# Mamba-2 decay rows read back from DRAM in place of TensorE broadcasts, and a gate moved ahead of two copies

## The reference, cut to what matters

```
adt  = dt * a                      # one value per token and head
a_cs = cumsum(adt, axis=-1)        # inside each chunk of 128
decay  = exp(segsum(adt))          # a_cs[l] - a_cs[s] for l >= s
y_diag = (C B^T * decay) @ xg
states = B @ (xg * exp(a_cs[-1] - a_cs))
y_off  = (C @ previous state) * exp(a_cs)
```

## Time and profile before

| | us |
|---|---|
| median of 3 runs (lowest, highest) | 2133.89 (2132.24, 2136.08) |
| profiled execution: its own time | 2128.42 |
| profiled execution: span of its instructions | 2126.6 |
| PE busy | 1967.8 (93%) |
| DVE busy | 1157.7 (54%) |
| ACT busy | 757.1 (36%) |
| POOL busy | 613.2 (29%) |

### The profile page before, as it was taken

One profiled execution on the slowest core, in us unless ns is written; L12 is line 12 of the kernel. 1 busy time (PEld: TensorE's weight loads), 2 busy tenths in 40 slices (PEclk: granted clock), 3 DMA queues, 4 the chain that ended last, 5 costly groups with the idle time before them and its releaser, 6 DMA issues.

```text
span 2126.6 us, 27616 instructions
## 1 busy us (share of the span) xinstructions
PE 1967.8 (93%) x10964; PEld 982.9 (46%) x10964; DVE 1157.7 (54%) x2320; ACT 757.1 (36%) x1345; POOL 613.2 (29%) x630
## 2 busy tenths in 40 slices
PE   2999889998999999989999899899999999999896
PEld 2443344454444455534444566544444444444542
DVE  6418999999995456422545688620233333332516
ACT  2413444314312866213321344331233333333503
POOL 0022415544446002478311322511101222022240
PEclk8999999999999999999999999999999999999998
DMA  8110111022311002331311100211111011100301
GB/s 336 40 45 25 50 40 50 21 85 75 129 79 69 37 11 85 139 119 40 128 40 40 40 1 1 79 40 40 41 41 41 1 41 41 41 10 32 120 20 79
DMA packets 18225, 127.10 MB, mean 60 GB/s; under 512 B 1744, under 2 KB 1744, under 8 KB 12848
## 3 DMA queue, kind: packets, MB, share of 16 engines
q1 hardware_dynamic: 12720, 97.57, 12.1%
q0 software_dynamic: 5376, 27.76, 3.3%
HBM read 106.45 MB, written 18.87 MB: 59 GB/s over the span
## 4 chain that ended last, share of the span: by engine, by line
PE 75%; DVE 14%; ACT 4%; POOL 3%; DMA 2%; issue 2%; SPq 0%; DVEq 0%; POOLq 0%; ACTq 0%
PE ps L871 48%; PE ps L868 7%; DVE arena L1631 3%; POOL arena L570 2%; PE ps L986 1%; PE ps L1223 1%; PE ps L921 1%; PE ps L963 1%; PE ps L969 1%; PE ps L908 1%; PE ps L1243 1%; PE ps L1088 1%; PE ps L936 1%; DMA W<-in_mods 1%; DVE arena L1847 1%
## 5 line engine op out<-in xcount | busy, mean ns | idle before, releaser
L871 PE MATMUL ps<-hT,W 128*128 128x512 bf16 x3456 | 812.3, 389 | 23.0 <-DVE arena L2150 7.2
L871 PEld LDWEIGHTS ps<-hT,W 128*128 128x128 bf16 x3456 | 327.6, 97 | 465.6 <-issue 34.9
L579 POOL TENSOR_TENSOR W<-W 128x512 bf16<-128x512 f32 x216 | 235.9, 1131 | 459.6 <-DMA W<-in_loads 458.3
L871 PE MATMUL ps<-W,arena 128*128 128x512 bf16 x1152 | 262.4, 388 | 8.8 <-DVE W L2016 6.2
L570 POOL TENSOR_TENSOR arena<-arena 128x512 f32<-128x512 f32 (+1 forms) x80 | 139.7, 1746 | 196.4 <-ACT arena L1569 126.4
L1409 ACT ACTIVATE arena<-arena,small 128x128 f32<-128x128 f32 (+9 forms) x192 | 114.1, 641 | 198.9 <-DVE small L1721 181.9
L871 PEld LDWEIGHTS ps<-W,arena 128*128 128x128 bf16 x1152 | 111.1, 97 | 158.1 <-DVE W L2016 6.7
L1402 ACT ACTIVATE arena<-arena,small 128x128 f32<-128x128 f32 (+9 forms) x192 | 122.8, 640 | 122.8 <-DVE small L1710 87.3
L868 PE MATMUL ps<-arena,W 128*128 128x512 f32 (+1 forms) x320 | 142.0, 598 | 0.9 <-DVE arena L1767 0.9
L871 PE MATMUL ps<-arena,W 128*128 128x512 bf16 x576 | 132.3, 391 | 5.4 <-POOL arena L631 4.4
L1710 DVE CUSTOM_DVE_ANT_0 arena<-ps,arena 128x256 f32<-128x256 f32 (+7 forms) x128 | 62.1, 518 | 123.8 <-PE ps L969 109.4
(11 more groups left out here) (321 smaller groups left out, 2673.7 us busy)
## 6 DMA issues: line engine op xcount, KB each, us to landing
W<-in_loads SPq DMA_DIRECT2D x34, 2048.0 KB, 7.6
gates_scratch<-arena SPq DMA_DIRECT2D x32, 256.0 KB, 2.0
arena<-gates_scratch POOLq DMA_DIRECT2D x2, 4096.0 KB, 15.4
arena<-in_x SPq DMA_DIRECT2D x2, 2048.0 KB, 13.8
W<-in_mods SPq DMA_DIRECT2D x2, 2048.0 KB, 18.4
hT<-in_mods SPq DMA_DIRECT2D x2, 2048.0 KB, 28.8
arena<-in_x POOLq DMA_DIRECT2D x1, 4096.0 KB, 13.5
x_scratch<-arena POOLq DMA_DIRECT2D x8, 512.0 KB, 8.7
```

The lines of the kernel that those rows point to most:

```text
L579: last = nc.gpsimd.tensor_tensor(low(v), v, high(v), ALU.subtract)
L871: last = mm(o, left[:, :, a], right[:, :, b], start=(k == 0 and (a, b) == PRODUCTS[0]), stop=(k == steps - 1 and (a, b) == PRODUCTS[-1]))
```

## The change

- A unit `("sums", 0)` is put ahead of `xbc2`. At `ct` 8 PE makes with it the cumulated sums, the chunk totals, and the cumulated sums transposed (a row for each chunk and head): three fp32 matmuls. ACT copies all three out and makes both exponentials there; DVE's difference and ACT's exponential for `dte` move there too.
- SP stores the transposed sums to DRAM (128x128 fp32), waits for the store, and reads 8 rows of them back to all 128 partitions (512 KB) for each step: the first two at once, the other 14 behind the load of `zs1`, each after the difference of two steps before has been read.
- PE's 8 matmuls a step (L1223) are gone; the scores stay, as `chunk_scores`. DVE takes the difference from SBUF and waits for the scores only ahead of the masked scores.
- In `window_attention` on DVE, `extra(n)` (the gate of the next pair) comes before `v_copies(n)`.

```diff
+    a = first["xbc2"]
+    first = {name: u + (u >= a) for name, u in first.items()}
+    first["sums"] = a
+    units[a:a] = [("sums", 0)]
...
+            def sums_row(m):
+
+                if m >= 2:
+                    sp.wait_ge(s_dif, m - 1)
+                row = sums_dram[8 * m:8 * m + 8, :].rearrange("h l -> (h l)").unsqueeze(0).to_broadcast([P, 1024])
+                nc.sync.dma_start(sums_rows[m % 2].rearrange("p h l -> p (h l)"), row).then_inc(s_rows[m % 2], 16)
...
                 load(n)
                 name = LOADS[n - 1]
+                if name == "xbc2":
+                    sp.wait_ge(s_cume, 1)
+                    nc.sync.dma_start(sums_dram, sumsT).then_inc(s_sums, 16)
+                    sp.wait_ge(s_sums, 16)
+                    sums_row(0)
+                    sums_row(1)
+                if name == "zs0":
+                    for m in range(2, 16):
+                        sums_row(m)
...
+                if name == "sums":
+
+                    pe.wait_ge(s_dtv, 3)
+                    mm(ps[:, unit_bank(u), 0:128], tri, adt, start=True, stop=True)
+                    mm(ps[:, unit_bank(u), 128:256], ones, adt, start=True, stop=True)
+                    mm(ps[:, unit_bank(u), 256:384], adt, tri, start=True, stop=True).then_inc(s_unit, 1)
                     return
...
-            pe.wait_ge(s_dtv, 3)
             pe.wait_ge(s_xs, 10)
-            mm(ps[:, 7, 0:128], tri, adt, start=True, stop=True)
-            mm(ps[:, 7, 128:256], ones, adt, start=True, stop=True).then_inc(s_cum, 1)
-
-            def decay_rows(m):
+
+            def chunk_scores(m):
                 c, g = m // 2, m % 2
                 if m:
                     pe.wait_ge(s_dif, m)
-                for h in range(8):
-                    a = adt[:, c * 16 + g * 8 + h:c * 16 + g * 8 + h + 1].to_broadcast([P, P])
-                    mm(ps[:, 2 + h // 4, (h % 4) * P:(h % 4 + 1) * P], a, tri, start=True, stop=True)
                 mm(ps[:, 4, 0:P], BTf[:, g, c * P:(c + 1) * P], CTf[:, g, c * P:(c + 1) * P], start=True,
                    stop=True).then_inc(s_csb, 1)
...
+                if ct == 8:
+                    evacs("sums")
+                    act.wait_ge(s_dtv, 4)
+                    A(dte, dte, ACT.Exp).then_inc(s_cume, 1)
...
+                    extra(n)
                     if n in V_TURNS:
                         v_copies(n)
-                    if n < len(items):
-                        extra(n)
...
-                dve.wait_ge(s_csb, m + 1)
+                dve.wait_ge(s_rows[m % 2], 16 * (m // 2 + 1))
                 if m >= 2:
                     dve.wait_ge(s_yd, m - 1)
                 d = decay[m % 2]
-                link(V.tensor_tensor(d, ps[:, 2:4, :].rearrange("p a (h l) -> p (a h) l", h=4),
-                                     per_head(cst, m, CHUNK), ALU.subtract))
+                link(V.tensor_tensor(d, sums_rows[m % 2], per_head(cst, m, CHUNK), ALU.subtract))
                 V.tensor_scalar(d, d, 0.0, None, ALU.min)
+                dve.wait_ge(s_csb, m + 1)
                 mult(cbm[m % 2], ps[:, 4, 0:P], tri).then_inc(s_dif, 1)
```

More of the change, by code:

```diff
@@ L180, in bank_before, with layer_kernel @@
     return None
-def layer_kernel(nc, x, mods, loads, params, consts, rows, alibi, out, x2_dram, gates_dram, q_dram):
+def layer_kernel(nc, x, mods, loads, params, consts, rows, alibi, out, x2_dram, gates_dram, q_dram, sums_dram):
     ctx = ExitStack()
@@ L290, in layer_kernel @@
         cbm = [area(27648, 128), area(29312, 128)]
+        sums_rows = [area(29440 + 1024 * s, 1024, "p (h l) -> p h l", h=8) for s in range(2)]
         yt = area(27776, 1024)
@@ L334, in layer_kernel @@
         dtr, dtv, adt, cst, ecs, dte, ctot = (small_junk[:, 128 * q:128 * q + 128] for q in range(7))
+        sumsT = small_junk[:, 896:1024]
         aexp = little(16)
@@ L412, in layer_kernel @@
         s_xs = sem("channels_placed")
-        s_cum = sem("decay_sums_made")
+        s_sums = sem("decay_sums_stored")
+        s_rows = [sem(f"decay_rows_loaded{i}") for i in range(2)]
         s_cume = sem("decay_sums_copied")
@@ L826, in unit @@
                 name, i = UNITS[u]
-                n = LOADS.index(name) if name != "dt" else None
+                n = LOADS.index(name) if name in LOADS else None
                 whole = name in WHOLE
-                if name != "dt" and i == 0 and share != 1:
+                if name in LOADS and i == 0 and share != 1:
                     if whole:
@@ L844, in unit @@
                     last.then_inc(s_unit, 1)
+                    return
+                if name == "sums":
[3 more added lines that the diff above has]
+                    mm(ps[:, unit_bank(u), 256:384], adt, tri, start=True, stop=True).then_inc(s_unit, 1)
                     return
@@ L1205, in _ @@
                     units("dt")
+                if ct == 8:
+                    units("sums")
                 if ct >= 2:
@@ L1230, in _ @@
             pe.wait_ge(s_dtv, 4)
-            decay_rows(0)
+            chunk_scores(0)
             unit(FIRST["zs0"])
@@ L1235, in _ @@
                 if m + 1 < 16:
-                    decay_rows(m + 1)
+                    chunk_scores(m + 1)
                     unit(FIRST["zs0"] + m + 1)
@@ L1351, in evac @@
                     last = A(dtT[0:16, half], bank[0:16], ACT.Copy) if i < 2 else A(dtr, bank[:, 0:128], ACT.Copy)
+                elif name == "sums":
+                    A(cst, bank[:, 0:128], ACT.Copy)
+                    A(dte, bank[:, 128:256], ACT.Copy)
+                    A(sumsT, bank[:, 256:384], ACT.Copy).then_inc(s_cume, 1)
+                    A(ctot, bank[:, 128:256], ACT.Exp)
+                    last = A(ecs, bank[:, 0:128], ACT.Exp)
                 elif name[:3] == "xbc":
@@ L1551, in _ @@
             act.wait_ge(s_x2st, 16 * NT)
[L1552 to L1557, removed]
             def gated_squares(m):
@@ L1721, in window_attention @@
                         V.reciprocal(rden[:, two], den[:, two]).then_inc(sems["inverse"], 1)
+                    if n < len(items):
+                        extra(n)
                     if n in V_TURNS:
                         v_copies(n)
-                    if n < len(items):
-                        extra(n)
             dve.wait_ge(s_par, 16)
@@ L2079, in _ @@
                     steps()
+                if ct == 8:
+                    dve.wait_ge(s_cume, 1)
+                    V.tensor_tensor(dte, dte, cst, ALU.subtract).then_inc(s_dtv, 1)
                 dve.wait_ge(s_free, conv_ready(ct))
@@ L2098, in _ @@
             V.memset(hst, 0.0).then_inc(s_st, 1)
-            dve.wait_ge(s_cume, 1)
-            V.tensor_tensor(dte, ps[:, 7, 128:256], cst, ALU.subtract).then_inc(s_dtv, 1)
             dve.wait_ge(s_cume, 2)
@@ L2339 @@
     queries = nc.dram_tensor("query_scratch", (P, 4 * SEQ), _mybir.dt.float32, kind="Internal").ap()
-    layer_kernel(nc, *args, out, x2, gates, queries)
+    sums = nc.dram_tensor("sums_scratch", (P, P), _mybir.dt.float32, kind="Internal").ap()
+    layer_kernel(nc, *args, out, x2, gates, queries, sums)
     r = _run(nc, [arrays], core_ids=[0])
```

## The result

| | before | changed |
|---|---|---|
| median us (lowest, highest) | 2133.43 (2132.24, 2136.08) | 2118.67 (2115.68, 2122.94) |
| profiled execution, its time; span | 2128.42; 2126.6 | 2115.68; 2113.9 |
| PE busy | 1967.8 | 1943.4 |
| DVE busy | 1157.7 | 1172.9 |

The ratio is 0.9931, with a 95% interval of 0.9911 to 0.9950: 14.8 us less by the medians. Forecast were 19.5 less, with a range of 2096 to 2124. The direction, the range and, as the chain shows, the mechanism held; the saving was a quarter smaller, and 2118.67 lies just above the narrower range of 2110 to 2118 that the prediction gave its own case.

A forecast was written before the change was run, and what follows sets the result against it. PE bounds the kernel before; in the chunk steps DVE colliding with GpSimd was to take over. Gains of 10.9 (steps), 2.5 (start) and 6.1 (gate) sum to 19.5 us: 2133.9 - 19.5 = 2114.4, range 2096 to 2124.

The forecast's parts named there:

- its own case: Whole kernel: DVE's collision with POOL sets the chunk step; 2114.4 us, own range 2110 to 2118, chance 0.6.
- 14 chunk steps: Chunk stage: broadcasts leave PE, steps fall from 10.91 to 10.13 us on average; gain 10.9 us, bounds 10.2 to 11.8.
- start of the stage: First chunk step: PE starts earlier, split collisions delay the second unit; gain 2.5 us with the 0.67 paid.
- sums at `ct` 8: Ahead of the chunk stage: three fp32 matmuls of 0.22 us join the path, costing 0.67 us.
- gate: Pair stage, item 8j-1: gate ahead of the copies cuts PE's wait by 1.01 us, six times; gain 6.1 us.
- PE leaves the chain, DVE and GpSimd take it: Chunk steps: PE's step falls to 9.12 us, so DVE colliding with POOL sets it at 10.07 to 10.18.
- The size of the step: Chunk steps: 7.37 us of DVE work plus 2.81 or 2.70 of collision, giving 10.18 or 10.07 us.
- the bad bound: Start of the chunk stage: the second wait halves PE's clock again, leaving a gain of 0.5 us.
- The lag is handed back at the end: End of the chunk stage: DVE falls behind PE, and the last step starts from its delayed instruction; no cost priced.
- Row loads: Rival, chunk stage: loads to all partitions set the step; 2163 us at 25 us a load, chance 0.05.
- PE's clock in the steps: Rival, chunk stage: waits of about 1 us a step lower the clock, stage gains nothing; 2125.3 us, chance 0.08.
- PE as the bound: Rival, chunk stage: the collision dissolves and PE still sets the step; 37 us gained, 2096.9 us, chance 0.15.

The follow-up runs named there:

- refill: Changed kernel with 4 of the 8 broadcast matmuls of each step put back on PE, results unread: ratio 0.9931 to the kernel before, same as the changed kernel.
- half_product: Changed kernel with GpSimd masking the decays of only 4 of 8 heads a step, the rest left out: ratio 0.9864 to the kernel before.
- reorder: Changed kernel with DVE's step reordered so that GpSimd's product meets instructions with PSUM operands: ratio 0.9858 to the kernel before.
- hold: Changed kernel with DVE waiting for GpSimd's split of zs1 before making the second step's inputs: ratio 0.9916 to the kernel before.
- both: Changed kernel with the new DVE order and the wait for the split together: ratio 0.9833 to the kernel before, median 2099.95 us.
- rows_twice: Changed kernel with every row load made twice, the second after the first landed, DVE waiting for both: ratio 0.9948 to the kernel before.
- rows_only: Changed kernel with the gate put back behind the copies of turned v: ratio 0.9972 to the kernel before, median 2127.21 us.
- gate_only: Kernel before with only the next pair's gate moved ahead of the copies of turned v: ratio 0.9961, median 2124.46 us.
- before_reorder: Kernel before with the new order of DVE's instructions in a chunk step: ratio 0.9987, median 2130.89 us.

## Why the prediction was right, and where its sizes were off

The terms, as forecast and as the two profiled executions show them (gain positive):

| term | forecast | measured | how read |
|---|---|---|---|
| 14 chunk steps | 10.9 | 9.6 | end of first step to last diagonal product: 1202.85 to 1358.66, and 1204.85 to 1351.04 |
| start of the stage, third matmul not counted | 3.2 | 0.5 | end of the last turned channels to end of first step: 1172.41 to 1202.85, and 1174.87 to 1204.85 |
| sums at `ct` 8 | -0.67 | -0.67 | 1127.34 to 1128.01 in the timeline after |
| last step | 0 | -1.9 | last diagonal product to next unit: 7.86 and 9.76 |
| gate | 6.1 | 6.0 | waits of 7.2 and 1.2 |
| sum | 19.5 | 13.5 | |

Two terms came out below the bounds that the prediction gave them: the chunk steps at 9.6 us (10.2 to 11.8), and the start, with the 0.67 taken off, at -0.2 (0.5 to 6.0).

- **PE leaves the chain, DVE and GpSimd take it.** Right, and shown by `refill` (0.9 us of PE work back a step, same time) and by `half_product` and `reorder` (both at 9.13 us a step).
- **The size of the step.** Forecast were 10.07 and 10.18 us, measured 10.17 and 10.32. I took 0.07 of overlap between a held instruction and the next off the step; there is none, the next starts 0.02 after (1232.75 + 2.93 to 1235.70). From the start of the held skip product to the next instruction it is 2.95 us for the 2.81 forecast, and the rest of that step is the 7.37 forecast. With 0.10 in the steps of the other kind it is 1.4 to 2.0 us over 14 steps, where the term is short by 1.3.
- **The start.** The step "at 0.56 us a collision and some six of them, the split ends at about 1191.2" was mis-sized: the split grew by 4.4 us and not 3.4, and began 2.9 later than before and not 0.7, of which about 1.8 had come about before the change's first instruction. What I had only as the bad bound, that the second wait lowers the clock again, is what happened: PE waited 4.03 us and its next unit took 6.83 instead of 5.4. So the first step ended at 1204.85 and not near 1200. `hold` shows that the collisions are the cause of most of the wait: with fewer of them it is 1.82 us. What the clock makes of the wait is less certain. The unit behind took 5.6 us after waits of 1.82 (`hold`) and 2.57 (`refill`), 7.13 after 2.54 (`both`), and 6.83 to 8.26 after waits of 4.0 to 4.8 (changed, `reorder`, `half_product`, `rows_twice`).
- **The last step.** "The lag is handed back at the end" was right as a mechanism, and was priced at nothing. But while DVE works off its lag, PE has nothing at all: it waits 6.37 us instead of 2.95, and then runs the last step at 1.2 GHz. In the five kernels with waits of 6.4 to 7.3 us (changed, `rows_only`, `refill`, `hold`, `rows_twice`) the diagonal product took 3.65 us each time. With waits of 2.8 to 3.1 it took 1.97 in four (before, `gate_only`, `before_reorder`, `both`) and 3.65 in two (`reorder`, `half_product`). So behind the long wait the product took 1.7 us more each time, and behind the short one in two kernels of six. In the kernel before the clock fell too, but only behind the product: the two groups after it took 1.57 and 1.91 us for 1.08 and 1.02.
- **The gate.** Right in place and size: 6.0 us by the waits, 6.4 by the length of the pair stage.
- **Row loads, PE's clock in the steps, PE as the bound.** The loads land in 3.5 us and can be doubled; the clock was 1.00 over the stage with waits of PE of 9.3 us in 11 steps, 1.0 at most. PE was not the bound, since in every step the collision held either the skip product or the state product behind it.
- **The rest.** Profile against profile the kernel gained 12.7 us, the terms give 13.5. Other stretches moved both ways, and nothing ties them to the change. The part ahead of its first instruction took 1.8 us more, and the 384 matmuls of one output stretch 88.20 us (granted clock 0.98) for 86.59 (1.00). The part behind the last gate's tanh took 145.3 us (0.95) for 147.5 (0.90), and in `gate_only` 149.6 (0.90).

The Trainium skill, page "SBUF — State Buffer", section "SBUF: two separate sides", says that GpSimd and a DVE instruction with two SBUF inputs exclude each other, for the whole of the first one. The runs agree for the skip and state products, and for those with a PSUM operand, which run free (0.68 us beside GpSimd in `reorder`). The clamp, with one SBUF input, was held too: beside the split at the start of the changed kernel it took 1.41 us for 0.69. On the length they differ a little: the second is held for 0.16 us less than the first lasts (1.10 of 1.26, 2.19 of 2.35).

## What to carry to other kernels

When work is taken from the engine that fills a step, add up the next engine's step with everything that now falls together, not its busy time today: here DVE's 9.13 us of mean busy time looked like PE's new 9.12, and the step became 10.25 us once no idle time absorbed the collision with GpSimd. If two engines exclude each other, put the instructions that are exempt beside the long one; moving two products, skip and state, in DVE's order was worth as much as the whole change, but only after it. And price the edges: the waits that grew at the start and the end of the stage were followed by half clock for a time in most of these kernels, and so were paid twice.

## What was not expected of the hardware

- A read of the same 4 KB from DRAM to all 128 partitions (512 KB) lands in 3.5 us, 3.2 to 4.7, faster than the 11.2 us that a load of the same size of constant rows took in the earlier trace rows; those were issued by another queue.
- PE's clock behind a wait is not the same in each kernel: the same 16 matmuls took 3.65 us in `reorder` and 1.97 in `both`, both after 2.79 us, and a unit took 5.58 us in `refill` (after 2.57) and 7.13 in `both` (after 2.54). What decides it stays open.
- A difference with both operands in SBUF takes the 1.22 us that it took with one in PSUM, where it does not meet GpSimd; beside the split it took 2.06.
